# Key pages scored two pairs at a time between the pages of even pairs, with an earlier release of the bank of a tile of k

## The reference

```python
k_past = cache_k[page_table]                      # (8 samples, 8 pages, 128 tokens, 8 heads, 128)
lg_sel = jnp.einsum('bqhd,bqhrkd->bqhrk', q, sel_k) * scale
p = jax.nn.softmax(jnp.concatenate([lg_sel, lg_own], axis=-1), axis=-1)
```

## Time and profile before

| what | value |
|---|---|
| time, median of 3 runs | 909.8 us (907.96 to 910.47) |
| span of the profiled execution | 909.7 us |
| TensorE busy with matrix products | 896.8 us, 99% |
| VectorE, ScalarE, GpSimd busy | 622.7, 438.1, 64.7 us |
| mean granted clock of TensorE | 0.996 of full speed |

### The profile page before, as it was taken

How to read it: one execution, slowest core, us unless ns; L and a number is a source line. 1 busy time by engine, 2 the same in 40 slices (tenths; PEclk the granted TensorE clock), 3 DMA queues, 4 the chain that set the end, 5 groups by cost and what they waited for, 6 DMA issues and landing times.

```text
span 909.7 us, 18709 instructions
## 1 busy us (share of the span) xinstructions
PE 896.8 (99%) x7472; PEld 838.1 (92%) x7472; DVE 622.7 (68%) x1089; ACT 438.1 (48%) x826; POOL 64.7 (7%) x81
## 2 busy tenths in 40 slices
PE   9999999999999999999999999999999999999996
PEld 8999988999999999999888878987999999999985
DVE  6477568788976575677575847446578897757536
ACT  5445666476345363445344453345447644526421
POOL 0010006500000000330000000000230000000000
PEclk9999999999999999999999999999999999999999
DMA  9982215664454444566988997998944545454401
GB/s 285 265 250 95 94 48 138 188 196 140 140 178 146 139 142 159 167 219 231 334 292 282 360 373 283 399 400 352 284 144 144 179 132 195 148 169 148 139 1 59
DMA packets 132331, 182.78 MB, mean 201 GB/s; under 512 B 5875, under 2 KB 113211, under 8 KB 132244
## 3 DMA queue, kind: packets, MB, share of 16 engines
q1 hardware_dynamic: 126938, 177.56, 59.0%
q0 software_dynamic: 640, 2.10, 0.9%
q10 hardware_dynamic: 4666, 1.92, 0.8%
HBM read 175.24 MB, written 6.32 MB: 200 GB/s over the span
## 4 chain that ended last, share of the span: by engine, by line
PE 94%; DMA 2%; SPq 1%; ACT 1%; DVE 1%; issue 1%; DVEq 0%
PE ps L624 24%; PE ps L626 23%; PE ps L625 23%; PE ps L1019 7%; PE ps L1061 4%; PE ps L1119 2%; DMA page<-in_cache_v_dram 2%; PE ps L907 1%; PE ps L909 1%; PE ps L908 1%; SPq L535 1%; SPq L542 1%; DMA x_tok<-in_x_prompt_dram 1%; PE ps L638 1%; PE ps L741 0%
## 5 line engine op out<-in xcount | busy, mean ns | idle before, releaser
L1232 ACT ACTIVATE w_hi<-raw 128x1024 fp32r<-128x1024 f32 x192 | 202.4, 1057 | 227.2 <-PE ps L626 204.4
L1636 DVE TENSOR_TENSOR w_lo<-raw,w_hi 128x1024 fp32r<-128x1024 f32 x192 | 237.4, 1240 | 102.7 <-ACT w_hi L1232 102.6
L624 PE MATMUL ps<-x_hi,w_hi 128*128 128x322 f32 (+1 forms) x888 | 279.8, 315 | 0.0
L626 PE MATMUL ps<-x_hi,w_lo 128*128 128x322 f32 (+1 forms) x888 | 276.5, 311 | 0.0
L625 PE MATMUL ps<-x_lo,w_hi 128*128 128x322 f32 (+1 forms) x888 | 276.1, 311 | 0.0
L624 PEld LDWEIGHTS ps<-x_hi,w_hi 128*128 128x128 f32 x888 | 168.1, 189 | 5.2 <-ACT k_turned L1523 2.9
L624 PE MATMUL ps<-h_hi,w_hi 128*128 128x320 f32 x552 | 170.9, 310 | 0.0
L626 PE MATMUL ps<-h_hi,w_lo 128*128 128x320 f32 x552 | 170.5, 309 | 0.0
L625 PE MATMUL ps<-h_lo,w_hi 128*128 128x320 f32 x552 | 170.4, 309 | 0.0
L625 PEld LDWEIGHTS ps<-x_lo,w_hi 128*128 128x128 f32 x888 | 168.8, 190 | 0.2
L626 PEld LDWEIGHTS ps<-x_hi,w_lo 128*128 128x128 f32 x888 | 167.6, 189 | 0.0
(11 more groups left out here) (347 smaller groups left out, 978.7 us busy)
## 6 DMA issues: line engine op xcount, KB each, us to landing
raw<-in_w_up_dram SPq DMA_DIRECT2D x32, 1024.0 KB, 5.8
raw<-in_w_down_dram SPq DMA_DIRECT2D x32, 1024.0 KB, 5.2
page<-in_cache_k_dram SPq DMA_DIRECT2D x64, 512.0 KB, 5.7
page<-in_cache_v_dram SPq DMA_DIRECT2D x64, 512.0 KB, 9.4
raw<-in_w_in_a_dram SPq DMA_DIRECT2D x11, 1024.0 KB, 8.7
raw<-in_w_kv_dram SPq DMA_DIRECT2D x8, 1024.0 KB, 6.6
raw<-in_w_out_a_dram SPq DMA_DIRECT2D x4, 1024.0 KB, 5.2
raw<-in_w_q_b_dram SPq DMA_DIRECT2D x4, 1024.0 KB, 5.4
```

Source lines behind the costliest of these rows:

```text
L624: mm(out, WH[PLACE[t]][:, k, :], hi[:, k, 0:width], start=(k == 0), stop=False)
L626: last = mm(out, WL[PLACE[t]][:, k, :], hi[:, k, 0:width], start=False, stop=(k == 7))
L1232: A(WH[PLACE[t]][:, :, :], raw_tile(t), ACT.Copy)\
L1636: V.tensor_tensor(WL[PLACE[t]][:, :, :], raw_tile(t), WH[PLACE[t]][:, :, :].bitcast(F32), ALU.subtract)\
```

## The change

The scores of a pair are no longer made after every pair. In an even pair from 2 on, the two pairs before it are scored in one visit, between its first and its second page; pairs 30 and 31 are scored after the loop. Odd pairs are turned without any score. Besides, the bank of a tile of k counts as read once the first pass on VectorE is done (`s_kb`).

```diff
@@ slot_read
-            return (s_uk, 8 + n + 1) if (p - K_FIRST) % 2 == 0 else (s_tc, n + 1)
+            return (s_kb, n + 1) if (p - K_FIRST) % 2 == 0 else (s_tc, n + 1)
@@ TensorE, key pages
                 turn_page(2 * pair)
+                if pair % 2 == 0 and pair:
+                    score_pair(pair - 2)
+                    score_pair(pair - 1)
                 turn_page(2 * pair + 1)
-                if pair >= 1:
-                    score_pair(pair - 1)
                 if K_FIRST <= pair <= K_FIRST + 16:
                     k_extra(pair)
+            score_pair(NPG // 2 - 2)
             score_pair(NPG // 2 - 1)
@@ VectorE, kvq
-                own(V.scalar_tensor_tensor(u[:, :], nmu[:, :], bank[:, T:T + 1], bank[:, 0:T], ALU.mult, ALU.add))
+                ins = V.scalar_tensor_tensor(u[:, :], nmu[:, :], bank[:, T:T + 1], bank[:, 0:T], ALU.mult, ALU.add)
+                if 8 <= i < 16:
+                    ins.then_inc(s_kb, 1)
+                    dve.wait_ge(s_kb, i - 7)
+                else:
+                    own(ins)
                 V.tensor_tensor(u[:, :], u[:, :], rs[:, :], ALU.mult).then_inc(s_uk, 1)
```

More of the change, by code:

```diff
@@ L384, in build @@
         s_nm = sem("new_m")
+        s_kb = sem("k_bank_read")
         s_out = sem("stored")
```

## The result

The changed kernel takes 912.55 us (median of 20 runs, 910.53 to 918.55), and the kernel before, run beside it, 910.47 us (20 runs, 907.55 to 915.08). The ratio is 1.0035, with a 95% interval of 1.0026 to 1.0045: slower by 3.2 us (2.4 to 4.1), where 4.4 were forecast.

The account below looks back on a forecast made before the run. The prediction took the key pages to be bound by TensorE's string of work; -3.5 - 1.3 + 6.9 + 0.8 + 1.5 = +4.4 us gave 914.2 us, own range 912.5 to 916, 8-in-10 range 909.0 to 917.5.

Parts of the forecast that it names:

- turn3's wait: After eight tiles of k, TensorE stands 0.86 us for ScalarE's copy queued behind the bias pass: 6.9 us more.
- pair 16: At the last tile of k VectorE is 0.8 to 0.9 us late, and so is turn3: 0.8 us more.
- The bank: After each tile of k the 0.16 us wait for VectorE's second pass goes: 1.3 us less for eight tiles.
- `left_out` before page 44: Before page 44's second half TensorE waits for VectorE's copy of page 42, behind `left_out` and `biases`: 1.5 us more.
- A visit: Each costs 0.20 us for changing from pages to scores plus 0.05 at its end; 14 x 0.25 = 3.5 us less.
- The own scores: The own keys' scores then follow a page as a visit of their own, giving back one of 15 saved visits.
- The base: Time of the kernel before: span 909.7 us plus 0.1 us by which the median of the runs is above it.
- Costed at nothing: Even pages' copies are covered, SyncE's page loads come in time, and value pages pass the shift through to the end.
- The absorbing rival: Value pages absorb part, as TensorE waits 2.0 us there for pages from memory: +2.4 us, 912.2 us; chance 0.05.
- No stall: The chain to turn3 is hidden and VectorE keeps up, leaving only the gains: 905.0 us; chance 0.12.
- half a stall: ScalarE's copy goes ahead of the bias pass; turn3 waits 0.35 us, eight times 2.8: 910.1 us; chance 0.12.
- further behind: In odd pairs the second score waits for VectorE's copy, 0.35 us for eight visits, 2.8 more: 917.0 us; chance 0.07.

Follow-up runs that it names:

- with the copy ahead: The changed kernel with ScalarE's copy of the next page moved ahead of the tile's bias pass: 908.99 us, ratio 0.9978 against the kernel before.
- the run without tiles: The kernel before with two pairs per visit only from pair 20 on and `left_out` after page 44: 908.24 us, ratio 0.9992.
- the run with turn3 later: The changed kernel with turn3 one page later: 914.30 us; with ScalarE's copy ahead of the bias pass as well: 907.22 us.
- the last version: The changed kernel with copy before bias pass, turn3 one page later, `left_out` after page 44, rebuild after copy, stores after next copy: 904.25 us.

## Why the prediction was right, and what was off

The direction and the mechanism were right: the change removes scores that hid waits, and the waits cost more than the visits. The size was too high: 2.8 us of the stretch where 4.4 were forecast. The difference is 0.6 less at turn3 and the bank, 0.1 less at page 44 and 0.9 more gained by fewer visits. By steps:

- **turn3's wait**: 8 times 0.86 plus 0.8 in pair 16, 7.7 us, were forecast, the part of a tile of k being the trace's own chain. Measured: 6.8 at turn3 and 0.3 at the bank, 7.1. turn3 loads 434.67 - 432.04 = 2.63 us after the tile's end, where 2.66 were forecast. That the copy's place behind the bias pass costs about half of it is shown: with the copy ahead 0.42 us go each time. The rule that ScalarE's queue is strictly first in, first out (the Trainium skill, TensorE: Matmul & The Clock Gate, Architectural detail) agrees with both runs. In pair 16 turn3 came 3.28 us after the tile's end, where 1.80 + 0.86 + 0.8 = 3.46 were forecast.
- **The bank**: the trace's 1.3 us went as forecast, but are worth nothing in the changed order: without the early signal the stretch is the same. The prediction said that turn3's wait swallows them and counted them on both sides, which is consistent. Alone they are worth 0.44, since later copies take back the rest.
- **`left_out` before page 44**: 1.5 forecast, 1.38 measured.
- **A visit**: the term that was mis-sized, 3.5 us forecast and 4.4 measured. The end of a visit was priced too low. It was taken from the two scores at the end of the earlier trace rows, 1.95 us, as 0.05. But there the second score waits for the copy of page 63, which ends at 547.05 + 0.69 = 547.74 us, and loads at 547.86; "0.33 <- issue" hides it. Two scores without such a wait take 1.86 to 1.87 us, so the end gives 2 x 1.00 - 1.87 = 0.13. The change from pages to scores gives a little less than the 0.20 forecast: two runs of 1.90 us become one of 532.19 - 528.55 = 3.64, which is 0.16. Together a visit gives 0.29 in the plain cycles and in the run without tiles; with a tile it gives 9.90 + 0.81 - 0.16 - 10.19 = 0.36. The own scores, given back at 0.25, take 511.54 - 509.93 - 0.85 = 0.76 us instead of 0.45, 0.31 more. Eight cycles at 0.36 and seven at 0.29 less 0.31 are 4.6, near the 4.4 of the account. That own scores after a page pay for a change of their own is what the Trainium skill (TensorEngine Tiling (Array Packing), Key Properties) says of a change of the tiling mode, and these rows agree.
- **The base**: the forecast stood on a median of 909.8 us from three runs; with twenty it is 910.47, 0.7 more. That moves the forecast's time, not its difference. For the time this was luck: with 910.47 as the base the forecast would have been 914.9 and its own range 913.2 to 916.7, above the measured 912.55.
- **Costed at nothing**: SyncE's wait until the first value page is 5.7 us in both, TensorE's for value pages 2.1 where it was 2.0, and the stretch behind is as long as before. The absorbing rival fell. "No stall" fell at the first turn3, "half a stall" by ScalarE's order, and "further behind" is not in the changed kernel and is in the run with turn3 later.

Open: why the granted clock before the key pages differs between executions, why a visit gives more where there is a tile of k, and why the issue of a store takes 1.65 or 1.99 us at some places. Not tried: the bias pass made shorter, or a fifth bank.

## What to carry to other kernels

Before small pieces of work are put together, look at what waits lie beneath each: a piece between two uses of a ring of buffers may be the cover for a reader on another engine, and its removal lays bare what it hid, here 0.81 us at each place against 0.3 for a visit. Then look at what stands ahead of that reader in its own engine's queue, a delayed pass or the issue of a store. Here the reader was put first and each late piece behind it, step by step, and that turned +2.8 us of the stage into -4.5. Take the price of a merged piece from a place where its second half waits for nobody, and check this against the rows of the other engines when a wait is labelled "issue".

## What the runs showed of the hardware

The issue of a store from ScalarE's queue holds up the compute instructions behind it. The two stores of the turned tile take 0.38 to 0.43 and 0.48 to 0.54 us in the changed kernel. In the run with turn3 later the second took 1.65 us at the place shown and 1.99 at another, and the copy behind it started at 438.52, 0.11 us after its end. In each of the eight cycles of that run the copy starts 0.10 or 0.11 us after the second issue. In the last version the issue began at 437.99 while a copy ran from 437.97, and the two went on beside each other.

The own scores' 32 loads after a page take 0.49 us, and the next page loads 0.58 us after the first of them (510.96 to 511.54). Before the first score of a visit the loads stand 0.16 to 0.20 us in every row shown, whether 16 or 32 loads of scores follow, and before the page after it 0.41 us, after 16 loads as after 32.
